# A two-layer hybrid trunk: the opening's wide weights in four parts instead of two halves

## The reference

```
def reference(x, c, w_ada, b_ada, norm_w, w_in, ...):
    c_act = jax.nn.silu(c)
    for l in range(DEPTH):
        mod = c_act @ w_ada[l] + b_ada[l]
        x = _layer(x, mod, norm_w[l], w_in[l], ...)
    return _rmsnorm(x, final_norm_w)

def _layer(x, mod, norm_w, w_in, ...):
    shift, scale, gate = jnp.split(mod, 3, axis=-1)
    h = _rmsnorm(x, norm_w) * (1.0 + scale[:, None]) + shift[:, None]
    proj = h @ w_in
    ...
```

## Time and profile before

| what | value |
|---|---|
| median of three runs | 1134.92 us (1134.83 to 1135.31) |
| profiled execution, its own time | 1134.01 us |
| span of its trace | 1132.3 us |
| PE busy | 1112.1 us, 98% of the span |
| DVE, POOL, ACT busy | 660.6, 561.7, 532.6 us |
| first wide matmul starts | 21.48 us |
| first matmul of the tile-by-tile end (`wide_end`) | 52.80 us |

### The profile page before, as it was taken

How to read it: one execution, slowest core, us unless ns; L and a number is a source line. 1 busy time by engine, 2 the same in 40 slices (tenths; PEclk the granted TensorE clock), 3 DMA queues, 4 the chain that set the end, 5 groups by cost and what they waited for, 6 DMA issues and landing times.

```text
span 1132.3 us, 15212 instructions
## 1 busy us (share of the span) xinstructions
PE 1112.1 (98%) x5807; PEld 917.6 (81%) x5807; DVE 660.6 (58%) x830; ACT 532.6 (47%) x930; POOL 561.7 (50%) x412
## 2 busy tenths in 40 slices
PE   6999999999999999999999999999999999999997
PEld 5778888888888888888898788888788887888885
DVE  4716465668788545538870635664887854131365
ACT  5544266655545533224462535666546553232234
POOL 5535444535445546545914363445355535464455
PEclk8999999999999999999999999999999999999999
DMA  9656423234443456653304463224433523443332
GB/s 322 208 134 197 132 76 93 76 112 131 129 119 84 129 177 199 206 156 104 96 20 101 142 205 93 76 75 120 130 99 99 132 73 87 116 133 94 105 100 93
DMA packets 203481, 140.79 MB, mean 124 GB/s; under 512 B 12001, under 2 KB 191249, under 8 KB 203409
## 3 DMA queue, kind: packets, MB, share of 16 engines
q1 hardware_dynamic: 202632, 138.91, 42.5%
q10 hardware_dynamic: 776, 0.91, 0.3%
HBM read 136.64 MB, written 2.63 MB: 123 GB/s over the span
## 4 chain that ended last, share of the span: by engine, by line
PE 95%; DVE 2%; SPq 1%; DMA 1%; issue 0%; POOL 0%; ACT 0%; DVEq 0%; POOLq 0%
PE main L683 77%; PE psC L683 6%; PE psA L683 5%; PE psB L683 4%; SPq L398 1%; DMA big<-in_w_ada 1%; PE psB L916 1%; PE psB L896 1%; DVE h_lo L1552 1%; SPq L426 0%; DVE psC L1505 0%; DVE tmp L1547 0%; PE psC L925 0%; POOL tmp L627 0%; DVE tmp L1505 0%
## 5 line engine op out<-in xcount | busy, mean ns | idle before, releaser
L601 POOL TENSOR_TENSOR w_lo<-raw,w_hi 128x512 fp32r<-128x512 f32 x344 | 502.3, 1481 | 537.4 <-ACT w_hi L1101 537.2
L683 PE MATMUL main<-h_hi,w_hi 128*128 128x512 f32 x976 | 388.7, 399 | 3.1 <-ACT h_hi L1101 2.9
L683 PE MATMUL main<-h_hi,w_lo 128*128 128x512 f32 x976 | 379.5, 390 | 0.0
L683 PE MATMUL main<-h_lo,w_hi 128*128 128x512 f32 x976 | 379.3, 390 | 0.0
L1101 ACT ACTIVATE w_hi<-raw 128x512 fp32r<-128x512 f32 x344 | 199.9, 623 | 286.1 <-PE main L683 161.8
L683 PEld LDWEIGHTS main<-h_hi,w_hi 128*128 128x128 f32 x976 | 183.6, 188 | 49.4 <-issue 11.1
L683 PEld LDWEIGHTS main<-h_hi,w_lo 128*128 128x128 f32 x976 | 183.2, 188 | 38.9
L683 PEld LDWEIGHTS main<-h_lo,w_hi 128*128 128x128 f32 x976 | 183.3, 188 | 38.0 <-issue 1.9
L1874 DVE TENSOR_TENSOR tmp<-main,misc 128x512 f32<-128x512 f32 x32 | 22.1, 692 | 165.3 <-PE main L683 162.8
L1713 DVE SCALAR_TENSOR_TENSOR misc<-main,cols,misc 128x511 f32<-128x511 f32 (+2 forms) x96 | 71.9, 749 | 60.9 <-ACT misc L1101 58.3
L683 PE MATMUL main<-y_hi,w_hi 128*128 128x512 f32 x256 | 100.5, 393 | 0.0
(11 more groups left out here) (288 smaller groups left out, 1411.8 us busy)
## 6 DMA issues: line engine op xcount, KB each, us to landing
raw<-in_w_in SPq DMA_DIRECT2D x124, 512.0 KB, 3.9
xbc<-in_w_ada SPq DMA_DIRECT2D x16, 512.0 KB, 4.9
zs<-in_w_ada SPq DMA_DIRECT2D x16, 512.0 KB, 4.6
raw<-in_w_pc SPq DMA_DIRECT2D x16, 512.0 KB, 3.8
raw<-in_w_out SPq DMA_DIRECT2D x16, 512.0 KB, 3.6
zs<-in_w_ada SPq DMA_DIRECT2D x16, 256.0 KB, 7.6
xbc<-in_w_in SPq DMA_DIRECT2D x8, 512.0 KB, 7.6
big<-in_w_ada SPq DMA_DIRECT2D x16, 256.0 KB, 7.2
```

Source lines behind the costliest of these rows:

```text
L601: nc.gpsimd.tensor_tensor(lo_b[:, cut, :], raw_b[:, cut, :], hi_b[:, cut, :].bitcast(F32), ALU.subtract).then_inc(s_split[b], 2 * BT_ // kt)
L683: return nc.tensor.matmul(o, a, b_, start=start, stop=stop)
```

## The change

The weights of the six tiles now travel in four parts of two slices each, part q behind quarter q in SP's order. The second and third couple lie side by side in `xbc`, so that one DMA of 512 KB brings a part of both (rows of 2 KB instead of 1 KB), and one of 256 KB that of the first couple; both count on one semaphore per part, and ACT waits for both. ACT's copies and POOL's splits are made per couple and part: three copies and three splits of 512 elements per partition for each part, twelve of each in all as before. The order on ACT, POOL and PE follows the parts. PE takes the low parts of all six tiles in one go also in pair 0. The loads of the fourth couple wait until part 3 of the first couple is split.

```diff
@@ sync
-            def wide(half):
-
-                cut = slice(half * BT_, (half + 1) * BT_)
-                for u in range(U_GA):
-                    sp.dma_start(couple_raw[u][:, cut, :], w_in_t[0, :, cut, u * 2 * P:(u + 1) * 2 * P]
-                                 ).then_inc(s_rawx[u][half], 16)
+            def wide(part):
+
+                cut = slice(2 * part, 2 * part + 2)
+                sp.dma_start(couple_raw[0][:, cut, :], w_in_t[0, :, cut, 0:2 * P]).then_inc(s_rawx[part], 16)
+                sp.dma_start(xbc[:, KT + 2 * part:KT + 2 * part + 2, :], w_in_t[0, :, cut, 2 * P:6 * P]
+                             ).then_inc(s_rawx[part], 16)
...
-            quarter(0)
-            wide(0)
-            quarter(1)
-            quarter(2)
-            wide(1)
-            quarter(3)
+            for q in range(QUARTERS):
+                quarter(q)
+                wide(q)
...
                 if (l, u) == (0, U_GA):
-                    for e in range(2):
-                        sp.wait_ge(s_split[e], part_count(0, 0, 1, e))
+                    sp.wait_ge(s_splitw, couple_count(0, KT - 1))
@@ gpsimd
+            def split_wide(part):
+
+                cut = slice(2 * part, 2 * part + 2)
+                for u in range(U_GA):
+                    pool.wait_ge(s_hiw, couple_count(u, 2 * part))
+                    nc.gpsimd.tensor_tensor(couple_lo[u][:, :, cut, :],
+                                            couple_raw[u][:, cut, :].rearrange("p k (b n) -> p b k n", b=2),
+                                            couple_hi[u][:, :, cut, :].bitcast(F32), ALU.subtract).then_inc(s_splitw, 1)
@@ scalar
+            def wide_hi_part(part):
+
+                cut = slice(2 * part, 2 * part + 2)
+                for u in range(U_GA):
+                    act.wait_ge(s_rawx[part], 32)
+                    f(couple_hi[u][:, :, cut, :], couple_raw[u][:, cut, :].rearrange("p k (b n) -> p b k n", b=2), ACT.Copy
+                      ).then_inc(s_hiw, 1)
...
-            def products(q):
+            def products(q, ks=None):
```

More of the change, by code:

```diff
@@ L209, in build @@
         s_raw, s_split = sem2("raw_loaded"), sem2("w_split")
-        s_rawx = [[sem(f"raw_wide_loaded{u}{half}") for half in range(2)] for u in range(3)]
+        s_rawx = [sem(f"raw_wide_loaded{part}") for part in range(QUARTERS)]
         s_hi = sem2("w_hi_done")
@@ L309, in build @@
         couple_raw = [raw[:, :, :, :].rearrange("p b k n -> p (b k n)").rearrange("p (k n) -> p k n", n=2 * P)] + [
-            xbc[:, KT + 4 * i:KT + 4 * i + 4, :].rearrange("p a (k n) -> p (a k) n", n=2 * P) for i in range(2)]
+            xbc[:, KT:CT, i * 2 * P:(i + 1) * 2 * P] for i in range(2)]
+        couple_hi, couple_lo = ([h[:, :, :, :]] + [t[:, 4 * i:4 * i + 4, :].rearrange("p (b a) (k n) -> p b (a k) n", b=2, n=P)
+                                                   for i in range(2)] for h, t in ((w_hi, y_hi), (w_lo, y_lo)))
         wide_ps = [main[0][:, :], main[1][:, :], psA[:, 0:512], psA[:, 512:1024], psB[:, 0:512], psB[:, 512:1024]]
@@ L358, in w_bufs, with couple_count @@
             return raw[:, b], w_hi[:, b], w_lo[:, b]
+        def couple_count(u, k):
+            return k // 2 * U_GA + u + 1
         def part_count(l, u, half, b):
-            if l == 0 and u < U_GA:
-                return u + 1 + U_GA * half
             return halves_before(l, u) + half + 1
         def wait_raw(eng, l, u, b, half):
[L368 to L371, removed]
+            eng.wait_ge(s_raw[b], (l * COUPLES + u - 2 - 2 * l) * 16)
         gate_slab = [xbc[:, 2 * i:2 * i + 2, :].rearrange("p a b -> p (a b)") for i in range(2)]
@@ L549, in _ @@
                             sp.dma_start(couple_raw[u + 1][:, cut, :], w_in_t[1, :, cut, u * 2 * P:(u + 1) * 2 * P]
-                                         ).then_inc(s_rawx[u][half], 16)
+                                         ).then_inc(s_rawx[2 * u + half], 16)
                     if m == 0:
@@ L630, in _ @@
                 if l == 0:
[L631 to L638, removed]
+                    for q in range(QUARTERS):
+                        split_wide(q)
+                        if q < QUARTERS - 1:
+                            add_products(q + 1)
                 for u in range(U_GA if l == 0 else 2, U_GA + 1):
@@ L809, in wide_high, with wide_low_weights @@
                 for i, (u, b) in enumerate(WIDE):
-                    pe.wait_ge(s_hi[b], part_count(0, u, k // BT_, b))
+                    pe.wait_ge(s_hiw, couple_count(u, k))
                     pe.wait_ge(s_hhi, k + 1)
                     mm(wide_ps[i], w_bufs(0, u, b)[1][:, k, :], h_hi[:, k, :], k == 0, False)
[L814 to L818, removed]
+            def wide_low_weights(k):
+                for i, (u, b) in enumerate(WIDE):
+                    pe.wait_ge(s_splitw, couple_count(u, k))
                     mm(wide_ps[i], w_bufs(0, u, b)[2][:, k, :], h_hi[:, k, :], False, False)
@@ L829, in wide_pair @@
                 a, b = 2 * q, 2 * q + 1
-                tiles = range(len(WIDE) - 1 if q == 0 else len(WIDE))
                 wide_high(a)
                 wide_high(b)
-                wide_low_weights(a, tiles)
+                wide_low_weights(a)
                 if q == 1:
                     quarter_sums(q + 1)
-                wide_low_weights(b, tiles)
+                wide_low_weights(b)
                 if q == 2:
@@ L1106, in w_hi_half @@
                     act.wait_ge(*free)
-                elif not is_wide(l, u):
+                else:
                     act.wait_ge(s_tile[b], 1 if (l, u) == (0, 3) else l * COUPLES + u)
@@ L1120, in pre_hi @@
                 raw_b, hi_b, _ = w_bufs(1, u, b)
-                act.wait_ge(s_rawx[u][half], 32)
+                act.wait_ge(s_rawx[2 * u + half], 48)
                 k = half * BT_
@@ L1186, in h_high @@
                 f(h_hi[:, k, tok], h_tmp[k % 4][:, tok], ACT.Identity, bias=mod[:, l, k:k + 1]).then_inc(s_hhi, 1)
-            def products(q):
-                for k in range(OWN[q]):
+            def products(q, ks=None):
+                for k in ks or range(OWN[q]):
                     act.wait_ge(s_ada[q % 2 * 4 + k // 2], (q // 2 + 1) * 32)
@@ L1199, in _ @@
             x_out()
-            for u, b in WIDE[:4]:
-                w_hi_half(0, u, b, 0)
+            wide_hi_part(0)
             h_high(0, 0)
             h_high(0, 1)
-            w_hi_half(0, 2, 0, 0)
-            w_hi_half(0, 2, 1, 0)
             products(1)
-            products(2)
+            wide_hi_part(1)
+            products(2, range(2))
             h_high(0, 2)
             h_high(0, 3)
-            for u, b in WIDE:
-                w_hi_half(0, u, b, 1)
+            products(2, range(2, OWN[2]))
+            wide_hi_part(2)
             h_high(0, 4)
```

10 lines of the change are left out of this document (5 added, 5 removed).

## The result

| kernel | median us | range, runs | ratio to before, 95% interval |
|---|---|---|---|
| before | 1134.77 | 1134.13 to 1135.31, 10 | |
| changed | 1138.39 | 1137.29 to 1139.15, 10 | 1.0031 (1.0023 to 1.0039) |

The change costs 3.6 us. The profiled execution of the changed kernel was the slowest of its ten, 1139.15 us with a span of 1137.4, against 1134.01 and 1132.3 before. So the two traces differ by 5.1 us, 1.5 more than the medians: one is of the slowest execution of its kernel, the other of one quicker than any in the table.

A forecast was written before the change was run, and what follows sets the result against it. PE, busy 98%, bounds the kernel, held in the opening by a ring through DVE, ACT and POOL. Cumulative lateness of 4.25 us at the tile-by-tile end, added to 1134.92, gives 1139.2 us, range 1135.8 to 1141.0.

The forecast's parts named there:

- a late tile-by-tile end: Close of the opening on PE: first tile-by-tile matmul at 57.05 against 52.80, 4.25 us late, carried through in full.
- pair 1: PE's matmuls after the sums of quarter 1: start at 33.8 against 34.27, 0.45 us won.
- pair 1 to the sums of quarter 2: PE waits for DVE, since POOL's additions wait for ACT's products behind `h_hi`; sums 0.85 us late.
- sums of quarter 2 to `h_hi` of slice 4: `h_low` of slices 2 and 3 is held by part 2's splits; `h_hi` at 43.9, pair 2 1.3 us late.
- `h_hi` of slice 4 to quarter 3 complete: Products and additions behind `h_hi` take 7.0 us as before; sums of quarter 3 at 50.9, 2.05 us late.
- quarter 3 complete to the last modulation, by way of `h_lo` of slices 4 and 5: DVE's `h_low` meets POOL's splits of part 3 and ends at 54.15; last modulation at 54.1.
- last modulation to the tile-by-tile end: Last link of the opening: 2.94 us as before, so the end comes at 57.05.
- The alternation: On DVE and POOL, `h_low` waits for the running split, the next split for `h_low`; rows of about 1.7 us.
- The lower bound, without contention: `h_low` on DVE not held up at all: tile-by-tile end at 53.7, 0.9 us late, 1135.8 us.
- The clock rival: A PE wait between full matmuls drops the clock to 0.50, costing 2.3 us: 1141.5 us; chance 0.08.
- The rival that ended on the other side: Only PE's old waits before the sums, pair 1 and the end go: 1.6 us won, 1133.3 us; chance 0.10.
- the ring: PE's sums, modulation, `h_hi`, ACT's products and POOL's additions feed the next sums; 3.22 us from sums to pair.

The follow-up runs named there:

- the kernel before with one line changed: Kernel before, with ACT making quarter 2's products of pieces 2 and 3 behind `h_hi` of slices 2 and 3; 1137.17 us, ratio 1.0022.
- the experiment with the wait ahead of part 2 alone: Changed kernel with POOL's splits of part 2 waiting until `h_low` of slice 3 is done, those of part 3 not; 1136.26 us, ratio 1.0017.
- both edits together: Changed kernel with ACT's products of quarter 2 all ahead of `h_hi` and POOL's splits of parts 2 and 3 behind `h_low`; 1134.75 us, ratio 1.0001.
- the kernel with the transfers of before: Changed kernel with parts 0 and 1 loaded behind quarter 0, parts 2 and 3 behind quarter 2; 1138.70 us, ratio 1.0035.
- the two experiments with POOL's waits alone: Changed kernel with POOL's splits held behind `h_low`: for parts 2 and 3, 1136.80 us; for part 2 only, 1136.26 us.
- The last two experiments: Changed kernel with more ACT products ahead of `h_hi`, POOL splits behind `h_low`, earlier quarter 1 sums: 1133.19 us; with quarter 3 added before part 2's splits: 1133.00 us.
- the first experiment: Changed kernel with all four of ACT's products of quarter 2 back ahead of `h_hi` of slices 2 and 3; 1136.13 us, ratio 1.0014.
- the second: Changed kernel with POOL's splits of part 2 waiting for `h_low` of slice 3, of part 3 for slice 5; 1136.80 us, ratio 1.0018.

## Why the forecast was right

It said 1139.2 (1135.8 to 1141.0), by a late tile-by-tile end, and 1138.39 was measured: 3.62 us late at the median, where 4.25 was forecast. The steps can be read only in the trace, which is of the slowest execution. They are counted from the first wide matmul, since that itself stood 0.49 us later:

| step | forecast | measured |
|---|---|---|
| pair 1 | 12.3 after the start | 12.81 |
| pair 1 to the sums of quarter 2 | 5.5 | 5.57 |
| sums of quarter 2 to `h_hi` of slice 4 | 4.6 | 4.35 |
| `h_hi` of slice 4 to quarter 3 complete | 7.0 | 7.00 (44.70 to 51.70) |
| quarter 3 complete to the last modulation, by way of `h_lo` of slices 4 and 5 | 3.2 | 3.09 (51.70 to 54.79) |
| last modulation to the tile-by-tile end | 2.94 | 3.01 |
| start to the tile-by-tile end | 35.6 | 35.83 |

The steps add up to both totals. The two mechanisms are the right ones. The order on ACT and the splits beside `h_low` were each taken away, which gave 2.3 and 1.6 us of the median, and with both taken away the median was that of before. The closeness of the total owes a little to luck: 0.5 us too little up to pair 1 stands against 0.25 and 0.1 too much further on.

The start at 21.97 was outside of what I had allowed (21.5). It is not of the change's making as far as the traces show: the kernel before with one line changed, which has the loads of before, started at 21.76, and the other experiments at 21.61 to 21.81. In the changed kernel's trace the pieces of quarter 0 that DVE waited for came about half a microsecond later.

**Contention between `h_low` and the splits.** The alternation that I read out of one case held: 3.20 and 3.25 for two that each meet a split already running, 1.41 with none. The first two taken singly (shortest, median and longest in ns, then first and last start):

```profile
L1557 DVE SCALAR_TENSOR_TENSOR h_lo<-tmp,mod,h_hi x2: 1507/1637/1767, 40.2 to 41.6; 128x512 fp32r<-128x512 f32 x2
```

The lower bound, without contention, did not come about. `h_32`, with an input in PSUM, took 1.41 for two at 20.32 although POOL's splits ran from 19.91. With that the trace agrees with the rule in the Trainium skill, page "GPSIMD Engine Reference", section "Key points", that the contention is with DVE instructions that have two SBUF inputs.

**The term that was mis-sized is the first.** I booked 0.45 us as won at pair 1. In the trace it is 12.81 after the start against 12.79 before: nothing. The step that was short is the 30 matmuls up to the sums of quarter 1: forecast 30.6 - 21.48 = 9.1, measured 31.55 - 21.97 = 9.58. From there to pair 1 it is 3.23, as forecast (3.22). The reason is how long the clock stayed low. In the changed kernel the window from 27 to 28 still shows 0.69, where the kernel before shows 1.00:

```profile
26.00:27.00 1.00, 1.00 (x4) 0.50 1.11 350
27.00:28.00 1.00, 1.00 (x5) 0.69 1.11 351
```

In the experiment with the wait ahead of part 2 alone the clock was at 1.00 from 26 on, and pair 1 started 33.45 - 21.74 = 11.71 after the start, 1.1 sooner than in the trace of before. Over the traces with the same order up to there, this term is worth between 0.2 lost and 1.1 won (12.97 in the trace of both edits together, 11.71 here). In the kernel before, the sums of quarter 1 wait for DVE anyway, which covers a later rise of up to 0.44 us. With the change nothing covers it. That may be why the changed kernel spreads over 1.9 us and the kernel before over 1.2. Of the 5.1 us between the two traces, 0.49 is the later start and 4.51 the way to the end; why the medians are only 3.6 apart is not shown.

**The clock rival came true, and in the changed kernel it cost nothing.** Behind the new wait of 1.24 us the granted clock fell. The windows of the changed kernel, and then of the kernel with the transfers of before, where the wait is 1.23 us:

```profile
41.00:42.00 1.00, 1.00 (x6) 0.64 0.50 106
42.00:43.00 1.00, 1.00 (x4) 0.50 0.66 86
43.00:44.00 1.00, 1.00 (x4) 0.50 0.10 14
```

```profile
42.00:43.00 1.00, 1.00 (x6) 1.00 0.52 63
```

Once it fell to 0.50, the lower level, once it stayed at 1.00, for the same wait. Pair 2 on PE was therefore late in the changed kernel: it started at 47.06, although ACT's `h_hi` had allowed it at 44.70 + 0.86 = 45.56, and the sums of quarter 3 stood at 52.50, 0.8 after they were complete. But the last modulation waited for `h_lo` until 54.79, and with 52.50 + 0.99 the sums were not the last to come. Both kernels need 35.83 us, and in both quarter 3 is complete 29.7 us after the first wide matmul. I had priced this case at 2.3 us more; the price was that of PE's time, and PE was not what was late at that place. This is shown for the changed kernel only. With one line changed in the kernel before, the fall cost about half a microsecond. In the two experiments with POOL's waits alone, executions with a lower mean clock took about 1.5 us longer, which points to a price of the fall there, though no trace shows one of them.

**The rival that ended on the other side** (only the old waits go) asked for ACT's products ahead of `h_hi`. The last two experiments gave it that and measured 1.5 and 1.7. That I had put 1.6 on it is chance as to the size: they had the splits out of the way and the sums of quarter 1 earlier as well, and with ACT's products of quarter 2 ahead alone (the first experiment) the kernel stayed 1.45 us over the one before.

The fourth couple's loads went out at 51.40, when the first split of part 3 was done, as forecast, and no wait for them shows. That all is carried through to the end is borne out by the 1079.4 to 1079.9 us behind the end in the traces of both kernels and of all experiments but the second.

## What to carry to other kernels

Where a result goes round through several engines before the matrix engine gets it back, look for the ring first, and check on every queue what a moved instruction now stands behind: two products behind two roundings cost 2.45 us here, and finer, earlier transfers showed no gain while that stood. Keep GpSimd's two-input work out of the stretches in which VectorE has instructions with two SBUF inputs on the critical path; an explicit wait can be the faster order. A price for a slower matrix engine counts only if it is the last to arrive at the next meeting. In the changed kernel it was not the last, in the kernel before with one line changed it was.

## What the runs showed of the hardware

- A VectorE instruction with two SBUF inputs and a GpSimd `tensor_tensor` took turns: where one started while the other ran, 0.75 us became 1.51 to 1.77, and GpSimd's 1.25 became 1.72 to 1.74 (the earlier trace rows and the line above).
- The granted clock can fall behind a wait of PE of 1.24 us, followed by 0.92 us of sums of one column, and can stay up behind one of 1.23. Of the five traces with such a wait before the sums of quarter 2 it fell in two (1.24 and 1.22) and stayed up in three (1.23, 1.23 and 1.24).
- While part 0, two thirds of it in 2 KB rows, came in, the loads ran at 374 GB/s in the changed kernel, against 347 with 1 KB rows. In all eight traces with parts this window shows 373 to 378:

```profile
16.00:17.00 1.00, 1.00 (x7) 0.50 1.05 374
```
